# Gated linear attention with both heads of a pair in one stationary block, second-half queries only, host-laid spatial weights and a ring of ten loads

## The reference, cut to what matters

```python
mod = silu(c) @ w_mod + b_mod                      # shift, scale, gate
h = rms_norm(x, g_pre) * (1 + scale) + shift
proj = h @ w_in                                    # 2048 x 5648, cut into the mixers' inputs
y_a = sliding_window_attention(...)                # 16 heads of 64
y_b = chunked_spatial_gating(gelu(s_u), gelu(s_v), sg_w, ...)   # 8 groups, weights 128 x 128 each
o_c = gated_linear_attention(c_q, c_k, c_v, log_alpha)          # 4 heads, keys of 64, values of 128
out = (concat(y_a, y_b, norm(o_c)) * silu(z)) @ w_out
x = x + gate * rms_norm(out, g_post)
```

## Time and profile before

| | |
|---|---|
| median of 3 runs | 3301.74 us (3298.95 to 3303.74) |
| profiled execution, its own time | 3298.99 us |
| its span, first to last instruction | 3297.2 us |
| PE / PEld / DVE / ACT / POOL busy | 91 / 76 / 58 / 45 / 2 % |
| mean granted TensorE clock | 0.969 |
| DMA | 608.9 MB, 185 GB/s |

### The profile page before, as it was taken

One profiled execution on the slowest core, in us unless ns is written; L12 is line 12 of the kernel. 1 busy time (PEld: TensorE's weight loads), 2 busy tenths in 40 slices (PEclk: granted clock), 3 DMA queues, 4 the chain that ended last, 5 costly groups with the idle time before them and its releaser, 6 DMA issues.

```text
span 3297.2 us, 36195 instructions
## 1 busy us (share of the span) xinstructions
PE 2986.3 (91%) x14132; PEld 2505.8 (76%) x14132; DVE 1922.3 (58%) x2432; ACT 1494.9 (45%) x2106; POOL 62.5 (2%) x69
## 2 busy tenths in 40 slices
PE   1598898799989889889999999998998999999998
PEld 1487777588768778668888888887876788888886
DVE  7887868785655444655554455444455555445544
ACT  0355434545445554455443444455553544344443
POOL 0000010000010000000000000000000000000000
PEclk9999899899999899989999999999998999999999
DMA  9885658684545445436655665554543565566554
GB/s 352 275 287 173 219 197 268 205 303 122 145 128 166 139 140 149 135 112 182 187 190 192 191 186 187 195 171 148 149 139 111 168 187 186 194 191 188 186 192 153
DMA packets 324314, 608.92 MB, mean 185 GB/s; under 512 B 19584, under 2 KB 77072, under 8 KB 323504
## 3 DMA queue, kind: packets, MB, share of 16 engines
q1 hardware_dynamic: 322336, 600.23, 57.5%
q0 software_dynamic: 1808, 6.38, 0.6%
HBM read 604.43 MB, written 2.10 MB: 184 GB/s over the span
## 4 chain that ended last, share of the span: by engine, by line
PE 61%; DVE 3%; ACT 2%; issue 1%; DMA 0%; DVEq 0%; POOL 0%; ACTq 0%
PE ps L1502 19%; PE ps L1504 19%; PE ps L1503 19%; PE ps L1482 1%; DVE w_lo L962 1%; PE ps L1523 1%; PE ps L1595 1%; ACT w_hi L697 1%; PE ps L1608 1%; ACT probs L841 0%; DVE x L972 0%; ACT hf L766 0%; DVE smax L1118 0%; DVE probs L1113 0%; ACT hf L760 0%
## 5 line engine op out<-in xcount | busy, mean ns | idle before, releaser
L962 DVE TENSOR_TENSOR w_lo<-raw,w_hi 128x1024 fp32r<-128x1024 f32 (+3 forms) x996 | 1158.4, 1169 | 1101.1 <-ACT w_hi L697 1098.7
L697 ACT ACTIVATE w_hi<-raw 128x1024 fp32r<-128x1024 f32 (+3 forms) x996 | 999.5, 1011 | 1272.2 <-PE ps L1504 1094.4
L1502 PE MATMUL ps<-w_hi,hT_hi 128*128 128x512 f32 (+2 forms) x2880 | 1131.6, 393 | 54.9 <-DVE w_lo L962 47.0
L1504 PE MATMUL ps<-w_hi,hT_lo 128*128 128x512 f32 (+2 forms) x2880 | 1104.3, 383 | 0.0
L1503 PE MATMUL ps<-w_lo,hT_hi 128*128 128x512 f32 (+2 forms) x2880 | 1103.1, 383 | 0.0
L1502 PEld LDWEIGHTS ps<-w_hi,hT_hi 128*128 128x128 f32 x2880 | 554.6, 193 | 154.7 <-issue 55.3
L1504 PEld LDWEIGHTS ps<-w_hi,hT_lo 128*128 128x128 f32 x2880 | 553.1, 192 | 94.5
L1503 PEld LDWEIGHTS ps<-w_lo,hT_hi 128*128 128x128 f32 x2880 | 554.8, 193 | 87.8 <-issue 1.9
L1502 PE MATMUL ps<-w_hi,uT_hi 128*128 128x512 f32 x1024 | 399.0, 390 | 0.0
L1503 PE MATMUL ps<-w_lo,uT_hi 128*128 128x512 f32 x1024 | 398.4, 389 | 0.0
L1504 PE MATMUL ps<-w_hi,uT_lo 128*128 128x512 f32 x1024 | 398.4, 389 | 0.0
(11 more groups left out here) (220 smaller groups left out, 1634.7 us busy)
## 6 DMA issues: line engine op xcount, KB each, us to landing
raw<-in_w_up SPq DMA_DIRECT2D x256, 512.0 KB, 3.6
raw<-in_w_down SPq DMA_DIRECT2D x256, 512.0 KB, 3.5
raw<-in_w_mod SPq DMA_DIRECT2D x192, 512.0 KB, 5.0
raw<-in_w_in SPq DMA_DIRECT2D x128, 456.0 KB, 3.5
raw<-in_w_in SPq DMA_DIRECT2D x112, 512.0 KB, 4.0
raw<-in_w_in SPq DMA_DIRECT2D x96, 344.0 KB, 3.6
raw<-in_w_out SPq DMA_DIRECT2D x64, 512.0 KB, 4.0
raw<-in_w_o SPq DMA_DIRECT2D x64, 512.0 KB, 3.5
```

The lines of the kernel that those rows point to most:

```text
L697: act.activation(w_hi[:, L % SPLIT_SLOTS, 0:c, 0:w], raw[:, G % RAW_SLOTS, 0:c, 0:w], ACT.Copy).then_inc(S.hi_ready, 1)
L962: dve.tensor_tensor(w_lo[:, r, 0:c, 0:w], raw[:, r, 0:c, 0:w], w_hi[:, s, 0:c, 0:w].bitcast(F32), ALU.subtract).then_inc(S.group_read, 1)
L1502: pe.matmul(o, a, wh, start=k0 + c == 0, stop=False)
L1504: mm = pe.matmul(o, b, wh, start=False, stop=k0 + c == job.chunks - 1)
```

## The change

Seven parts:

- The ring has ten slots instead of eight. Room for it comes from `sgw` and the smaller `levels` table.
- The host lays the spatial weights out transposed (`sg_wT`); GpSimd loads them straight into `sgwT`, after the second reciprocal root of the layer. TensorE's transposes and the two copies out of PSUM go; VectorE masks all eight in place with one instruction, behind the wait for the rows.
- The queries of a pair of heads are held twice, once with the lower and once with the upper partition half zeroed (`gq[:, 0]` and `gq[:, 1]`), and the keys once (`gk`). One product over all 128 partitions, with both heads' keys as the stationary block, gives both heads' scores.
- From level 1 on only queries of the second half of each block are made and moved: 64 of the 128 of a tile. A level's four products fill one bank, and VectorE empties it with one masked copy. Level 0 has four products of 256 columns in two banks; the last step two of 256 columns in one.
- From level 3 on GpSimd makes only the first-half keys, and of the last step only the first tile's.
- The distance is written with its final sign by two instructions, one per half, and ScalarE's Abs goes.
- The wait between the products of a level goes; a wait for the zeroed halves comes before level 0. In the second block the buffers `qrT`, `cT_hi` and `cT_lo` change places.

The diff, cut to its core (moved buffers of the second block, semaphore names and the list of inputs are left out):

```diff
 BIG = 1e30
-RAW_SLOTS = 8
+RAW_SLOTS = 10
 SPLIT_SLOTS = 4
...
     b = 2 ** n
-    lv.append((s // b == t // b) & (s % b < b // 2) & (t % b >= b // 2))
+    late = np.nonzero(np.arange(P) % b >= b // 2)[0][None, :]
+    lv.append((s // b == late // b) & (s % b < b // 2))
 levels = np.concatenate([m.astype(np.int32) for m in lv], axis=1)
...
 sgwT = A1s("sgwT", [P, SGG, P])
-sgw = A1("sgw", [P, SGG, P])
 sgln = A1("sgln", [P, 2, COLS])
 gq = A1k("gq", [P, 2, 2, 2 * P])
-qlev = A1k("qlev", [P, 2, 2, 2 * P])
+gk = A1k("gk", [P, 2, 2 * P])
+qlev = A1k("qlev", [P, 2, 2, 2, P])
 klev = A1k("klev", [P, 2, 2, 2 * P])
...
+def halves_of(v, lev):
+    b = v.rearrange("p k (b n) -> p (k b) n", n=2 ** lev)
+    return b[:, :, 0:2 ** lev // 2], b[:, :, 2 ** lev // 2:]
+def early(v, lev, all_of_it=False):
+    if lev > LEVELS:
+        return v[:, :, 0:P]
+    return v if all_of_it else halves_of(v, lev)[0]
 GLA_SLOTS = 3 + LEVELS + 1 + 3
...
              (gup[:], io["gla_w_gate_up"].rearrange("l r n -> r l n")),
-             (levels[:], io["levels"].rearrange("p (l n) -> p l n", n=P))):
+             (levels[:], io["levels"])):
 pool.dma_start(dst, src).then_inc(S.small_landed, 16)
...
 pool.wait_ge(S.swa_padded, 2 * l + 2)
-pool.dma_start(sgw[:], io["sg_w"][l].rearrange("g t s -> t g s")).then_inc(S.rows_landed, 16)
 pool.dma_start(sgln[:, 0], io["sg_ln_g"][l].partition_broadcast(P)).then_inc(S.rows_landed, 16)
...
 rsqrt(2)
+pool.dma_start(sgwT[:], io["sg_wT"][l]).then_inc(S.rows_landed, 16)
 for lev in range(1, LEVELS + 2):
     pool.wait_ge(S.gla_q, n(S.gla_q))
-    pool.tensor_tensor(klev[:, lev % 2], glf[:, lev % 2], gq[:, 1], ALU.mult).then_inc(S.gla_k, 1)
+    k, e, g = (early(v, lev, lev <= 2) for v in (klev[:, lev % 2], glf[:, lev % 2], gk[:]))
+    pool.tensor_tensor(k, e, g, ALU.mult).then_inc(S.gla_k, 1)
 rsqrt(8)
...
 bank_copy(cgT[:], 2 * P)
-bank_copy(gq[:, 0].rearrange("p k n -> p (k n)"), scale=GDK ** -0.5)
-yield
-bank_copy(gq[:, 1].rearrange("p k n -> p (k n)"))
+parts_copy([(0, GDK, gq[0:GDK, 0]), (GDK, P, gq[GDK:P, 1])], scale=GDK ** -0.5)
+yield
+bank_copy(gk[:].rearrange("p k n -> p (k n)"))
 act.wait_ge(S.gla_logits, l + 1)
...
     act.wait_ge(S.gla_k, l * (LEVELS + 1) + lev - 2)
-link(act.activation(f(gle[:, lev % 2]), f(gle[:, lev % 2]), ACT.Abs))
 act.activation(f(glf[:, lev % 2]), f(gle[:, lev % 2]), ACT.Exp, scale=-1.0 / 16).then_inc(S.gla_factor, 1)
...
 n(S.var_ready)
-for half in range(2):
-    b = dve_bank()
-    drained(dve.tensor_tensor(sgwT[:, 4 * half:4 * half + 4], ps[:, b].rearrange("p (g t) -> p g t", g=4),
-                              repeat(K["tril"], 4), ALU.mult))
 yield
...
 dve.wait_ge(S.rows_landed, rows_value(1, l))
+dve.tensor_tensor(sgwT[:], sgwT[:], repeat(K["tril"], SGG), ALU.mult)
 for t in range(TOK):
...
         n_b = 2 ** lev
-        g = glb[:].rearrange("p k (b n) -> p (k b) n", n=n_b)
-        mid = g[:, :, n_b // 2 - 1:n_b // 2].broadcast_to([P, 4 * P // n_b, n_b])
-        dve.tensor_tensor(e.rearrange("p k (b n) -> p (k b) n", n=n_b), g, mid, ALU.subtract
-                          ).then_inc(S.gla_dist, 1)
+        (g0, g1), (e0, e1) = halves_of(glb[:], lev), halves_of(e, lev)
+        mid = g0[:, :, n_b // 2 - 1:n_b // 2].broadcast_to([P, 4 * P // n_b, n_b // 2])
+        dve.tensor_tensor(e0, g0, mid, ALU.subtract)
+        dve.tensor_tensor(e1, mid, g1, ALU.subtract).then_inc(S.gla_dist, 1)
     else:
-        link(dve.tensor_tensor(e[:, :, 0:P], glb[:, :, 0:P],
-                               glb[:, :, P - 1:P].broadcast_to([P, 2, P]), ALU.subtract))
-        dve.tensor_copy(e[:, :, P:2 * P], glb[:, :, P:2 * P]).then_inc(S.gla_dist, 1)
+        dve.tensor_tensor(e[:, :, 0:P], glb[:, :, 0:P],
+                          glb[:, :, P - 1:P].broadcast_to([P, 2, P]), ALU.subtract)
+        dve.tensor_scalar(e[:, :, P:2 * P], glb[:, :, P:2 * P], -1.0, None, ALU.mult).then_inc(S.gla_dist, 1)
+def late_queries(lev):
+    q, e, o = gq[:], glf[:, lev % 2], qlev[:, lev % 2]
+    if lev <= LEVELS:
+        half = 2 ** lev // 2
+        q = q.rearrange("p v k (b n) -> p v (k b) n", n=2 * half)[:, :, :, half:]
+        o = o.rearrange("p v k (b n) -> p v (k b) n", n=half)
+        e = halves_of(e, lev)[1]
+    else:
+        q, e = q[:, :, :, P:2 * P], e[:, :, P:2 * P]
+    e = e.unsqueeze(1).broadcast_to([P, 2, e.shape[1], e.shape[2]])
+    dve.tensor_tensor(o, q, e, ALU.mult).then_inc(S.gla_q, 1)
...
-    for t in range(TOK if lev <= LEVELS else 1):
+    if lev > LEVELS:
         b = dve_bank()
-        if lev <= LEVELS:
+        drained(dve.tensor_copy(pairs[:, 2], ps[:, b]))
+    elif lev:
+        half = 2 ** lev // 2
+        b = dve_bank()
+        late = pairs[:, 0:2].rearrange("p t (h b n) -> p (t h) b n", h=GH, n=2 * half)[:, :, :, half:]
+        mask = levels[:, P + (lev - 1) * P // 2:P + lev * P // 2].rearrange("p (b n) -> p b n", n=half)
+        drained(dve.copy_predicated(late, mask.unsqueeze(1).broadcast_to([P, 2 * GH, P // 2 // half, half]),
+                                    ps[:, b].rearrange("p (g b n) -> p g b n", g=2 * GH, n=half)))
+    else:
+        for t in range(TOK):
+            b = dve_bank()
             drained(dve.copy_predicated(pairs[:, t].rearrange("p (h n) -> p h n", h=GH),
-                                        repeat(levels[:, lev], GH),
+                                        repeat(levels[:, 0:P], GH),
                                         ps[:, b].rearrange("p (h n) -> p h n", h=GH)))
-        else:
-            drained(dve.tensor_copy(pairs[:, 2], ps[:, b]))
...
                          ).then_inc(S.gla_logits, 1)
+dve.memset(gq[GDK:P, 0], 0.0)
+dve.memset(gq[0:GDK, 1], 0.0).then_inc(S.gla_padded, 1)
 link(dve.memset(pairs[:, 0:2], 0.0))
...
 dve.wait_ge(S.gla_factor, n(S.gla_factor))
-dve.tensor_tensor(qlev[:, lev % 2], glf[:, lev % 2], gq[:, 0], ALU.mult).then_inc(S.gla_q, 1)
+late_queries(lev)
 if lev + 2 <= LEVELS + 1:
...
 def spatial(l):
-    pe.wait_ge(S.rows_landed, rows_value(1, l))
-    for half in range(2):
-        b = dve_bank()
-        for j in range(4):
-            mm = pe.transpose(ps[:, b, j * P:(j + 1) * P], sgw[:, 4 * half + j], ident)
-        mm.then_inc(S.dve_bank_filled, 1)
     yield
...
 def level(lev):
-    q, k = gq[:, 0], gq[:, 1]
-    if lev:
-        pe.wait_ge(S.gla_q, n(S.gla_q))
-        pe.wait_ge(S.gla_k, n(S.gla_k))
-        q, k = qlev[:, lev % 2], klev[:, lev % 2]
-    for ts, tt in (((0, 0), (1, 1)) if lev <= LEVELS else ((0, 1),)):
-        b = dve_bank()
-        for h in (0, 2, 1, 3):
-            r = (h % 2) * GDK
-            if h == 1:
-                mm.then_inc(S.pe_step, 1)
-                pe.wait_ge(S.pe_step, n(S.pe_step))
-            mm = pe.matmul(ps[:, b, h * P:(h + 1) * P], k[r:r + GDK, h // 2, ts * P:(ts + 1) * P],
-                           q[r:r + GDK, h // 2, tt * P:(tt + 1) * P], start=True, stop=True)
-        mm.then_inc(S.dve_bank_filled, 1)
+    if lev == 0:
+        for t in range(TOK):
+            b = dve_bank()
+            n_ = slice(t * P, (t + 1) * P)
+            for kt in range(2):
+                mm = pe.matmul(ps[:, b, kt * 2 * P:(kt + 1) * 2 * P].rearrange("p (v n) -> p v n", v=2),
+                               gk[:, kt, n_], gq[:, :, kt, n_], start=True, stop=True)
+            mm.then_inc(S.dve_bank_filled, 1)
+        return
+    pe.wait_ge(S.gla_q, n(S.gla_q))
+    pe.wait_ge(S.gla_k, n(S.gla_k))
+    q, k = qlev[:, lev % 2], klev[:, lev % 2]
+    b = dve_bank()
+    tiles, width = (TOK, P // 2) if lev <= LEVELS else (1, P)
+    for t in range(tiles):
+        for kt in range(2):
+            at = (t * 2 + kt) * 2 * width
+            mm = pe.matmul(ps[:, b, at:at + 2 * width].rearrange("p (v n) -> p v n", v=2),
+                           k[:, kt, t * P:(t + 1) * P], q[:, :, kt, t * width:(t + 1) * width],
+                           start=True, stop=True)
+    mm.then_inc(S.dve_bank_filled, 1)
 act_done()
+pe.wait_ge(S.gla_padded, l + 1)
 level(0)
...
 arrays["lambdas"] = np.stack([a[k] for k in ("lambda_q1_2", "lambda_q2_2", "lambda_k1_2", "lambda_k2_2")], axis=1)
+arrays["sg_wT"] = a["sg_w"].transpose(0, 3, 1, 2)
 arrays["rel"] = a["rel_bias_2"][:, :, band()].transpose(0, 2, 1, 3)
```

## The result

The kernel after takes **3248.2 us** (median of four runs, 3245.2 to 3249.1), the kernel before 3301.5 in the same comparison: ratio 0.984, interval 0.982 to 0.985. That is 53 us less. The forecast was 26 less, with a range that ended at 3256: right in sign, half the size, and outside the range. The profiled execution took 3247.9 us, its span 3246.1, so it stands for the median.

A forecast was written before the change was run, and what follows sets the result against it. TensorE's own work plus short stalls, behind which the clock falls, was taken to bound the kernel. Terms -16.0 -7.2 -3.5 -3 -1 +4.5 = -26.2 us gave 3273 (3275.5 for a median); range 3256 to 3296.

The forecast's parts named there:

- Ring of ten: Weight loads: two more in flight save 3 us, bounds 0 and 8.
- Rival D: Load ring: ten slots do nothing because SP waits for TensorE, not room; 3278.5 us, chance inside the forecast's 0.64.
- Levels on TensorE: GLA level products and dropped weight transposes: 21.3 us of TensorE time, three quarters taken, 16.0 us less; bounds 10.6, 21.3.
- One bank per level: GLA levels: waits for the second bank behind modulation sums go, with some clock loss; 7.2 us less, bounds 3.7 and 10.
- The way to the operands: Stalls before level products: dropping Abs and halving key products saves 3.5 us, bounds 0 and 5.4.
- The opening: Kernel start: VectorE's wait for the smaller levels table shrinks, 1 us less, bounds 0 and 2.3.
- Spatial weights: Spatial gating, both layers: the later load makes VectorE, then TensorE, wait; 4.5 us more, bounds 2.2 and 11.4.
- VectorE, at nothing: VectorE's split distances, dropped masked copy, added memsets and short runs: no net cost or gain, 0 us.
- A: GLA stages: operands set the pace, TensorE's saved time turns into waits; only 6 us less, 3295.5 us, chance 0.17.
- C: Spatial load lands very late behind the ring's loads, slower from 18.7 us on; at 25 us, 3314 us, chance 0.05.
- B: GLA stages: shorter stalls return 14 us of half-clock loss, level term in full; 42 us less, 3260 us, chance 0.14.

The follow-up runs named there:

- a_rest: Changed kernel with ring of eight, spatial weights loaded at the layer's start, two banks and masked copies per level, Abs back, full key products: 3279.7 us, ratio 0.993.
- a_early8: Changed kernel with the spatial weights loaded at the layer's start and a ring of eight: 3261.1 us, ratio 0.988.
- a_early: Changed kernel with the spatial weights loaded at the layer's start into free columns of proj, ring of ten kept: 3240.6 us, ratio 0.981.
- a_ring8: Changed kernel with the ring back at eight slots, nothing else: 3269.0 us, ratio 0.990.
- a_dose: Changed kernel with every product of levels 1 to 8 done twice into the same place: 3262.0 us, ratio 0.988.
- a_early8_tb: Changed kernel with early spatial load, ring of eight, and two banks with two masked copies per level: 3268.9 us, ratio 0.991.
- a_klev: Changed kernel with GpSimd's key product over all keys at every level: 3251.6 us, ratio 0.984.

## Why the prediction was half right

From a_rest to a_early8 to a_early to the change there is a path from before to after on which each step is measured:

```
                                     predicted   measured
level products, transposes, opening      -17.0      -20.8   (before to a_rest)
one bank, Abs, half keys                 -10.7      -18.6   (a_rest to a_early8)
ring of ten                               -3.0      -20.5   (a_early8 to a_early)
spatial weights                           +4.5       +7.6   (a_early to after)
sum                                      -26.2      -52.3   (measured directly: -53)
```

**The failed step is "Ring of ten".** It took 3 us, with 8 as the bound, from the sentence "The 13.9 us of the earlier trace rows is the most that loads cost TensorE directly". The row above it, ScalarE's 138.5 us, I had put aside as "mostly hidden". The flaw is the word directly: the ring gave 19 to 21 us. ScalarE rounds weights and makes the factors of the levels and the tails of the other mixers in one order; a load that is late for its rounding delays all behind it, and what TensorE then waits for has another name in the waits (qlev, klev, a modulation sum), or none. The 13.9 didn't even fall: in the kernel after that row is 16.7 us. From a_ring8 to the kernel after it goes from 17.7 to 16.7, while all other waits of TensorE from 100 to 1090 us fall from 123.2 to 109.7. "Mostly hidden" was right for steady stretches, as in0 shows, and wrong for the starts of stages and the mixer pieces. Rival D, that the ring does nothing, was wrong in the same way: SP waits for TensorE, true, but for a group further back, and that is what a slot gives. The bound that would have held, though a loose one, is the whole of ScalarE's waits in the stages where it is late, and the row that pointed there was shown.

The ring makes up 17.5 us of the 26 that were missed. Some 8 more lie in the second row of the table, told below.

**Levels on TensorE.** 0.86 us by the row of the output step, 0.81 measured. If anything the share was off: three quarters taken, 11.2 to 13.8 of 13.8 us measured (a_dose), and with the full 21.3 and 1 for the opening it is -22.3, against -20.8 with 4.5 us to either side. The row had decided rightly against the rule of the Trainium skill, TensorEngine Tiling (Array Packing), "Performance Considerations": the full-height products took 0.81 us where the row halves with a wait between them took 2.23. No run takes out the wait alone, so how much of the 1.4 us is the wait's, and what 64-row products without it would cost, isn't shown.

**One bank per level.** 7.2 predicted, 6.6 and 7.8 measured (4.4 and 7.3 in block 1 of the traces), and by the mechanism named: undoing it brings back the row behind the modulation sums. **The way to the operands:** 3.5 predicted with 5.4 as the bound. Undone one by one, 1.9 and 3.4, neither told apart from nothing; undone together, with the old ring and two banks (a_rest against a_early8_tb), 10.8. So the term was too small on the path of the table, and what it is worth hangs on what else is in the kernel. **The opening:** 1 predicted, 1.4 in the table of stages.

**Spatial weights.** Right in kind, 7.6 us where 4.5 was taken, inside 2.2 to 11.4 (12.4 by block 1 of the traces). The landing of 7.0 us is near the 6.7 taken for layer 0, but layer 1 didn't land in 4.4, and GpSimd's rstd took 1.26 us in place of 0.70. The estimate of 3.2 us from the Trainium skill, DMA: Bandwidth & Descriptors, "Anatomy of one DMA", agrees with neither load here.

**VectorE, at nothing.** The prediction said that runs of one to eight words are no dearer. That holds for the distances and not for the masked copy: of levels 1 and 2, with runs of one and two words, it takes 1.30 to 1.33 us, of the later levels 0.69 to 0.74. Nor is a second distance always short, as told at the end. What the two cost in time isn't shown.

**The rivals.** A fell: the waits of level products went from 13.1 to 5.5 us in layer 0 and from 5.9 to 4.1 in layer 1. (All waits of the two GLA stages together stayed at 33 us, since the spatial product waits 9.6 us longer.) C fell at 7 us, far from its 18.7. B, the clock, had the nearest time (3260). The granted clock rose from 0.90 to 0.94 in layer 0, which is 160 x 0.10 - 135 x 0.06 = 8 us, and from 0.94 to 0.95 in layer 1, about 2 more, where B said 14 and the forecast had 3.5 in the bank's term. So B was right in part, and part of that came with the ring: in a_ring8 the clock of layer 0's stage is 0.92. B took the ring at 3 us like the forecast, and so its time is the nearest by luck.

## What to carry to other kernels

A ring's depth is to be counted against the buffer behind it, all kinds of loads counted: how long before the next stage can use an item is its load issued, and is that longer than a landing? Here a ring of eight left 0 to 2.5 us for landings of 4 to 5, and a ninth slot was worth 21 us, as much as all the work that was taken off TensorE; the tenth gave nothing that could be measured. Waits of an engine that is "not the bottleneck" are to be read for what stands behind them in its order; a direct wait of the bottleneck for the same cause is no upper bound. And a transfer that is moved later because its buffer is shared should first be offered other free room: here there was some, and it gave 7.6 us.

## What the runs showed of the hardware that was not expected

VectorE's second distance takes longer when it starts beside a GpSimd key product. In the kernel after, VectorE and GpSimd:

```profile
404.56 0.42 DVE L1218 TENSOR_TENSOR gle<-glb 128x256 f32<-128x256 f32 x1
404.73 0.85 POOL L670 TENSOR_TENSOR klev<-glf,gk 128x256 f32<-128x256 f32 x1 [4.88 <-DVE qlev L1236]
...
404.90 0.96 DVE L1219 TENSOR_TENSOR gle<-glb 128x256 f32<-128x256 f32 x1
...
405.78 1.31 DVE L1248 COPY_PREDICATED pairs<-levels,ps 128x512 f32<-128x512 int32 x1
```

The second distance has the first one's shape and takes 0.96 us instead of 0.42. The key product's record ends at 405.58, the distance's 0.28 later. In the kernel after, seven of the 14 second distances are long, and each ends 0.28 us behind the key product beside it: 0.95 to 0.96 us where that takes 0.85, 1.49 to 1.50 where it takes 1.4. In a_klev, where the key products of levels 3 to 5 take 1.41 instead of 0.85 us, the long distances beside them take 1.51 to 1.52. Where a second distance stays at 0.42 beside a key product, it is the key product that is long (1.70 and 1.75 us for 512 elements instead of 1.37 and 1.39). By these rows one of the two waits for the other to end (records of GpSimd are rough, but the pattern is the same in both kernels). The first distance, which begins before the key product, shows nothing of this.

The masked copy here takes 1.31 us for another reason: it is that of level 2, and those of levels 1 and 2 take 1.30 to 1.33 us in both layers, with a key product beside them or not, and as much in a_klev. Their runs of one and two words are the likely cause; no run changes them alone.

Block 2 comes in two lengths, 2204 or 2207 us, in variants of both kernels. The shorter ones have 88 to 95 us at the half clock in it, the longer ones 101 to 105. What decides between them isn't known.
